# Compression products of a trunk kernel spread over four 32-wide strips of TensorE, with fp32 score masks

## The chip, the cores and the metric

The kernel runs on one core of a Trainium2 chip. The metric is the device time of one execution in microseconds (us). Before the change the median of three runs is 2889.2 us (2888.13 to 2898.22).

## What is computed

A two-layer trunk on 512 tokens of width 2048 (batch 1). Each layer modulates its input, projects it with `w_in`, mixes tokens in three ways side by side (six heads of sparse attention, "NSA", in two key/value groups; six heads of a gated delta rule; four heads of stick-breaking attention), projects with `w_out` and normalizes. The change touches the NSA part. For each of the two groups of a layer:

```python
blk = kv[:, cidx] + pe                   # 31 blocks of 32 tokens, one block every 16 tokens, head dim 128
flat = blk.reshape(31, 32 * 128)
kc or vc = silu(flat @ w1) @ w2          # w1: 4096 x 128, w2: 128 x 128, once for keys, once for values
...
sc = q @ kc.T * scale                    # coarse scores, masked, softmax
ss = q @ ks.T * scale                    # scores on the selected keys, causal mask, softmax
sw = q @ kw.T * scale                    # scores on the window's keys, causal mask, softmax
```

With 512 tokens the selection holds all blocks and the window holds all tokens, so that both of the fine scores are 512 x 512 with a causal mask.

## The kernel before

**The work around the change.** Everything is fp32. The big projections are made of three products with fp32r operands (a high and a low part of each operand). Weights come in one stream: SyncE (SP) loads halves of 128 x 1024 numbers, 512 KB each, into a ring of four slots (`ring`, L391 to L394, in a hardware loop of four loads), and waits before each for its slot's semaphore `raw_free0` to `raw_free3`. For a weight tile GpSimd (POOL) copies a half into `w_hi` and subtracts to get `w_lo` (L1194, L1196), and then frees the slot; TensorE (PE) multiplies eight k-steps of three products by each half (`column_tile`, L450 to L452). A tile is two halves. ScalarE (ACT) copies the finished tile from PSUM (L843, `copy_group`).

**A group's order on PE** (a hardware loop over two groups in each of two layers, so four passes): tile 0 (keys to be compressed), tile 1 (values), `compress(0)`, `compress(1)`, tile 2, the turning of the hidden values, tile 3, the two small `w2` products, tiles 4 to 7, and then three heads, each in 11 steps, between which the remaining six tiles are spread. In the stream the eight halves of `w1` ("D" items: four for keys, four for values) stand behind the halves of tiles 0 and 1, one in each slot for `compress(0)`, then one in each for `compress(1)`, and behind them tiles 2, 3 and so on.

**compress(which)** (L531 to L535) makes 32 products, one for each token of a block: stationary 128 x 31 (`blocks_kv`, made by VectorE, DVE), moving 128 x 128 (`ring`), all added up in `TB[which][0:31]`. It waits for slot q4's load, makes that slot's eight products, and releases the slot:

```python
for q4 in range(4):
    pe.wait_ge(S(f"slot_in{q4}"), ...)
    for i in range(CMP_LEN // 4):
        t = q4 * (CMP_LEN // 4) + i
        last = mm(TB[which][0:N_CMP, 0:HD], blocks_kv..., ring[:, q4, ...], start=(t == 0), ...)
    last.then_inc(S(f"raw_free{q4}"), 1)
```

ACT takes tanh of the sum (L936), DVE makes the silu of it in `hidden` (L1363, L1364), PE turns it (L553) behind tile 2, DVE copies it to `cmpb` (L1367), and PE needs it behind tile 3 (L558).

**The fine scores** (L600, L601): for each head and each of its eight blocks of queries a product of q and keys, 128 x 128 to 128 x 512, and on its last 128 columns a second product that adds the causal mask, `ident_r` times `causal_r`. Both are fp32r copies of constants, which DVE makes once at the start (L1255, L1256). There are 2 layers x 6 heads x 8 = 96 such masks. DVE takes the maximum, ACT the exponential, DVE scales, PE turns (L621) and multiplies by the values (L629).

Of the kernel before, what the change touches and what calls it, by code (L numbers as in the profile page):

```python
# [18 lines left out]
P = 128  # L19
# [103 lines left out]
def constants():  # L123
# [26 lines left out]
    blocks["rot"] = rot  # L150
    inv = np.float32(ROPE_THETA) ** (-np.arange(ROPE_HALF, dtype=np.float32) * np.float32(2.0)
# [11 lines left out]
def build(nc, x, positions, c, b_mod, mod0, small_cols, stream, small, lns, const, out, where, layers=DEPTH):  # L163
    x_norm = nc.dram_tensor("x_norm", (TT, P, DM), F32, kind="Internal").ap()
    ctx = ExitStack()
    with ctx:
# [24 lines left out]
        ident_r = sb("ident_r", [P, P], F32R)  # L191
        causal_r = sb("causal_r", [P, P], F32R)
# [12 lines left out]
        hidden = sb("hidden", [N_CMP, 2, HD])  # L205
# [78 lines left out]
        hid_tanh = A(16, N_CMP)[:, 0:2 * HD].rearrange("p (a n) -> p a n", a=2)  # L284
# [131 lines left out]
        def _(pe):  # L416
# [56 lines left out]
            for l in range(layers):  # L473
# [41 lines left out]
                with pe.Fori(0, KVH) as g:  # L515
# [11 lines left out]
                    def compress(which):  # L527
                        pe.wait_ge(S("blocks_ready"), G * 2 + which + 1)
                        for q4 in range(4):

                            pe.wait_ge(S(f"slot_in{q4}"), (turn_of_group(l, g) + (which + 2)) * 16)  # L531
                            for i in range(CMP_LEN // 4):
                                t = q4 * (CMP_LEN // 4) + i
                                last = mm(TB[which][0:N_CMP, 0:HD], blocks_kv[which][:, t * N_CMP:(t + 1) * N_CMP],
                                          ring[:, q4, i * HD:(i + 1) * HD],  # L535
                                          start=(t == 0), stop=(t == CMP_LEN - 1))
                            last.then_inc(S(f"raw_free{q4}"), 1)
# [12 lines left out]
                    pe.wait_ge(S("hid_ready"), G * 2 + 2)  # L550
                    for which in range(2):

                        last = mm(SB_[which][:, 0:N_CMP], hidden[:, which, :], ident[0:N_CMP, 0:N_CMP],  # L553
                                  start=True, stop=True)
# [21 lines left out]
                    for r in range(GROUP):  # L576
                        H = G * GROUP + r
                        q = qT[r % 2]
                        for s in range(NSA_STEPS):
# [13 lines left out]
                            if 1 <= s <= 8:  # L593
# [7 lines left out]
                                mm(SB_[(u + 1) % 2][:, w - P:w], ident_r[:, :], causal_r[:, :],  # L601
# [238 lines left out]
        def _(act):  # L840
# [34 lines left out]
            for l in range(layers):  # L875
# [37 lines left out]
                with act.Fori(0, KVH) as g:  # L913
# [19 lines left out]
                    for which in range(2):  # L933

                        act.wait_ge(S("raw_free3"), after("raw_free3", turn_of_group(l, g) + (which + 2)))
                        fn(hid_tanh[:, which, :], TB[which][0:N_CMP, 0:HD], ACT.Tanh, scale=0.5)\  # L936
                            .then_inc(S("cmp_tanh"), 1)
                    copy_group(2, kS)
                    copy_group(3, v_raw[0])
                    act.wait_ge(S("cmp_done"), G + 1)  # L940
                    fn(cmpb[:, 0, 0:N_CMP], SB_[0][:, 0:N_CMP], ACT.Copy)
                    fn(vcmp[0:N_CMP, :], SB_[1][0:N_CMP, 0:HD], ACT.Copy)
# [293 lines left out]
        def _(dve):  # L1236
# [18 lines left out]
            cp(ident_r[:, :], ident)  # L1255
# [533 lines left out]
```

## Time and profile before

| | |
|---|---|
| three runs | 2889.2 us median (2888.13 to 2898.22) |
| profiled execution | 2894.21 us, span in the trace 2892.4 us, mean granted TensorE clock 0.959 |
| PE busy | 2557.2 us (88%) |
| PE weight loads | 2016.3 us (70%) |
| DVE busy | 1381.7 us (48%) |
| POOL busy | 1209.2 us (42%) |
| ACT busy | 646.9 us (22%) |
| HBM | 303.92 MB read, 108 GB/s over the span |

The page of the profile gives busy time by engine and, below, instructions in groups by line of the kernel. L843 and L1240 are lines of helpers through which all ACT and nearly all DVE instructions go, so their tiles tell them apart.
### The profile page before, as it was taken

What the parts mean: (1) busy time and instruction counts of PE and PEld (TensorE: products, weight loads), DVE (VectorE), ACT (ScalarE), POOL (GpSimd) and SP (SyncE); (2) the same over time, 40 slices, a digit from 0 to 9 for tenths busy, and PEclk for the clock granted to TensorE, in tenths of its full rate; (3) what the DMA queues carried; (4) which work ended last, traced back from release to release, by engine and by line L of the source; (5) the groups of instructions that cost most, each with busy time, mean ns of one, the idle gap of its engine ahead of it and who ended that gap; (6) DMA issues with size and microseconds to landing.
All of it is one profiled execution on the core that took longest, in us unless ns stands there. A gap on an engine that the chain in (4) does not pass through costs nothing.

```text
span 2892.4 us, 40548 instructions
## 1 busy us (share of the span) xinstructions
PE 2557.2 (88%) x14320; PEld 2016.3 (70%) x14320; DVE 1381.7 (48%) x1915; ACT 646.9 (22%) x1168; POOL 1209.2 (42%) x692
## 2 busy tenths in 40 slices
PE   0499879988999999998987999999899999997994
PEld 0387667666777777776875777777677777775784
DVE  8614751575555553564234143135555554447435
ACT  0201210112222222343003022012222222335000
POOL 7134234323333333544652533443333334443564
PEclk9999989998999999998998999999999999998997
DMA  9533443343111112445323311421111111335531
GB/s 360 220 115 109 135 151 124 124 146 109 59 59 59 60 62 73 157 152 171 95 69 116 124 60 53 131 66 52 59 59 59 59 59 59 124 131 167 184 107 73
DMA packets 82901, 314.81 MB, mean 109 GB/s; under 512 B 9974, under 2 KB 10230, under 8 KB 76950
## 3 DMA queue, kind: packets, MB, share of 16 engines
q1 hardware_dynamic: 76608, 295.51, 31.1%
q10 hardware_dynamic: 6108, 16.83, 1.6%
q8 instruction: 116, 1.90, 0.3%
q14 instruction: 69, 0.57, 0.1%
HBM read 303.92 MB, written 8.39 MB: 108 GB/s over the span
## 4 chain that ended last, share of the span: by engine, by line
PE 68%; DVE 18%; issue 5%; ACT 4%; POOLq 2%; DVEq 1%; ACTq 1%; DMA 0%; SPq 0%
PE bank L450 14%; PE bank L452 13%; PE bank L451 13%; DVE arena L1240 11%; DVE acc L1240 4%; PE bank L831 4%; PE bank L833 4%; PE bank L832 4%; PE bank L430 2%; ACT arena L843 2%; DVE tiny L1240 2%; PE bank L600 1%; ACT L843 1%; PE bank L629 1%; POOLq L1197 1%
## 5 line engine op out<-in xcount | busy, mean ns | idle before, releaser
L1194 POOL CAST w_hi<-ring 128x1024 fp32r<-128x1024 f32 (+1 forms) x328 | 347.4, 1059 | 1594.0 <-PE bank L452 1024.5
L450 PE MATMUL bank<-h_hi,w_hi 128*128 128x512 f32 x2048 | 889.0, 434 | 27.6 <-POOLq L1197 24.1
L452 PE MATMUL bank<-h_hi,w_lo 128*128 128x512 f32 x2048 | 819.5, 400 | 0.9 <-issue 0.9
L451 PE MATMUL bank<-h_lo,w_hi 128*128 128x512 f32 x2048 | 819.3, 400 | 0.0
L1196 POOL TENSOR_TENSOR w_lo<-ring,w_hi 128x1024 fp32r<-128x1024 f32 (+1 forms) x328 | 795.9, 2426 | 48.6 <-issue 2.2
L450 PEld LDWEIGHTS bank<-h_hi,w_hi 128*128 128x128 f32 x2048 | 397.9, 194 | 132.6 <-POOLq L1197 26.8
L452 PEld LDWEIGHTS bank<-h_hi,w_lo 128*128 128x128 f32 x2048 | 395.8, 193 | 90.7
L451 PEld LDWEIGHTS bank<-h_lo,w_hi 128*128 128x128 f32 x2048 | 398.0, 194 | 82.1 <-issue 13.5
L843 ACT ACTIVATE arena<-bank 128x512 f32<-128x512 f32 (+6 forms) x352 | 165.8, 471 | 969.2 <-PE bank L452 395.1
L831 PE MATMUL bank<-w_hi,h_hi 128*128 128x512 f32 x512 | 201.2, 393 | 1.9 <-POOLq L1197 1.9
L1240 DVE SCALAR_TENSOR_TENSOR acc<-ring,cact,acc 128x1024 f32<-128x1024 f32 x128 | 183.3, 1432 | 40.3 <-DMA ring<-in_stream 24.3
L833 PE MATMUL bank<-w_hi,h_lo 128*128 128x512 f32 x512 | 199.3, 389 | 0.0
L832 PE MATMUL bank<-w_lo,h_hi 128*128 128x512 f32 x512 | 199.2, 389 | 0.0
L1240 DVE TENSOR_TENSOR arena<-arena,cst 128x256 f32<-128x256 f32 (+3 forms) x160 | 107.2, 670 | 84.9 <-ACT last_CT L843 49.5
L430 PEld LDWEIGHTS bank<-arena 64*64 64x64 f32 x2880 | 95.2, 136 | 72.6 <-issue 55.9
L843 ACT ACTIVATE arena<-bank,tiny 128x512 f32<-128x512 f32 (+3 forms) x132 | 75.4, 571 | 313.3 <-DVE tiny L1240 286.6
L843 ACT ACTIVATE arena<-arena 128x512 f32<-128x512 f32 (+5 forms) x186 | 95.7, 515 | 208.7 <-DVE arena L1240 178.4
L430 PE MATMUL bank<-arena 64*64 64x64 f32 x2880 | 111.2, 224 | 26.8 <-DVEq L1554 20.0
L843 ACT ACT_TABLE_LOAD x91 | 116.8, 1283 | 68.5 <-issue 61.5
L1240 DVE SCALAR_TENSOR_TENSOR arena<-arena 128x512 f32<-128x512 f32 (+1 forms) x82 | 85.8, 1047 | 80.6 <-ACT arena L843 52.9
L1240 DVE TENSOR_TENSOR arena<-bank,yT 128x512 f32<-128x512 f32 x32 | 22.1, 692 | 212.5 <-PE bank L833 210.7
L831 PEld LDWEIGHTS bank<-w_hi,h_hi 128*128 128x128 f32 x512 | 96.1, 188 | 23.9 <-POOLq L1197 3.2
(192 smaller groups left out, 2756.5 us busy)
## 6 DMA issues: line engine op xcount, KB each, us to landing
ring<-in_stream SPq DMA_DIRECT2D x480, 512.0 KB, 3.6
yT<-in_mod SPq DMA_DIRECT2D x32, 1024.0 KB, 6.2
arena<-in_x SPq DMA_DIRECT2D x1, 4096.0 KB, 14.4
arena<-in_x ACTq DMA_DIRECT2D x4, 1024.0 KB, 10.0
x_norm<-arena ACTq DMA_DIRECT2D x4, 1024.0 KB, 9.3
arena<-x_norm ACTq DMA_DIRECT2D x4, 1024.0 KB, 9.5
out<-arena SPq DMA_DIRECT2D x4, 1024.0 KB, 3.9
raw<-in_lns ACTq DMA_DIRECT2D x8, 256.0 KB, 5.6
```

The costliest lines, as they stand in the source:

```text
L430: last = mm(dst[rows, t, :], lhs[rows, t, :], rhs[rows, t, :], start=True, stop=True)
L450: mm(PJ[b][:, :], hi, h_hi[:, k, :], start=(k == 0), stop=False)
L451: mm(PJ[b][:, :], hi, h_lo[:, k, :], start=False, stop=False)
L452: last = mm(PJ[b][:, :], lo, h_hi[:, k, :], start=False, stop=(k == KT - 1))
L600: mm(SB_[(u + 1) % 2][:, 0:w], q[:, w - P:w], keys[:, 0:w], start=True, stop=False)
L831: mm(outs[t][:, :], h_hi[:, k, at], hi, start=(k == 0), stop=False)
L832: mm(outs[t][:, :], h_hi[:, k, at], lo, start=False, stop=False)
L833: last = mm(outs[t][:, :], h_lo[:, k, at], hi, start=False, stop=(k == KT - 1))
L843: made = act.activation(*args, **kw)
L1194: pool.tensor_copy(w_hi[:, par, 0:w], ring[:, slot, 0:w])
L1196: pool.tensor_tensor(w_lo[:, par, 0:w], ring[:, slot, 0:w], w_hi[:, par, 0:w].bitcast(F32), ALU.subtract)
L1240: made = op(*args, **kw)
```

## The change

The 32 products of `compress` are dealt to four strips. Slot q4's eight products go to output partitions 32 x q4 to 32 x q4 + 30, four strips in turn, so that each strip holds the partial sum of one slot. PE waits for all four slots at once, and releases each with its strip's last product, all four at the end. ACT copies all 128 partitions of the partial sums to `cmp_part`; behind tile 2, in the place where `hidden` was turned, PE multiplies by the constant `sum4` (one in row r, column r mod 32), which adds the four strips and turns. ACT's tanh and one DVE instruction now work on the turned sum; the factor 0.5 moves into the copies behind the `w2` products. The masks are added by a product of the fp32 constants, and the two fp32r copies and their two DVE instructions go away. The constants grow by 31 columns.

```diff
@@ -148,6 +148,7 @@
         rot[ROPE_HALF + i, i] = -1.0
         rot[i, ROPE_HALF + i] = 1.0
     blocks["rot"] = rot
+    blocks["sum4"] = (row % 32 == col[:, :N_CMP])
     inv = np.float32(ROPE_THETA) ** (-np.arange(ROPE_HALF, dtype=np.float32) * np.float32(2.0)
                                      / np.float32(2 * ROPE_HALF))
     misc = np.zeros((P, 2))
@@ -188,8 +189,6 @@
         sm_all = sb("sm_all", [P, SMALL_W])
         cact = sb("cact", [P, 2, KT])
         modT = sb("modT", [P, 2, KT])
-        ident_r = sb("ident_r", [P, P], F32R)
-        causal_r = sb("causal_r", [P, P], F32R)
         h_mod = sb("h_mod", [P, 2, KT])
         ea = sb("ea", [P, GDN_H])
         gates = sb("gates", [P, TT, 18])
@@ -202,7 +201,7 @@
         meanvar = sb("meanvar", [P, TT, 2])
         cmpb = sb("cmpb", [P, 6, 32])
         vcmp = sb("vcmp", [P, HD])
-        hidden = sb("hidden", [N_CMP, 2, HD])
+        cmp_part = sb("cmp_part", [P, 2, HD])
 
         def C(name, parts=P):
             at, n = where[name]
@@ -281,7 +280,8 @@
         masked = [narrow(A(14)), narrow(A(14)[:, NW:])]
         lv_n = narrow(A(17))
         lastT = last_CT[:, :].rearrange("p (t n) -> p t n", t=TT)
-        hid_tanh = A(16, N_CMP)[:, 0:2 * HD].rearrange("p (a n) -> p a n", a=2)
+        hid_tanh = A(16)[:, 0:2 * N_CMP].rearrange("p (a n) -> p a n", a=2)
+        hid_sum = SB_[0][:, 0:64].rearrange("p (a n) -> p a n", a=2)[:, :, 0:N_CMP]
 
 
 
@@ -526,15 +526,17 @@
 
                     def compress(which):
                         pe.wait_ge(S("blocks_ready"), G * 2 + which + 1)
-                        for q4 in range(4):
-
+                        for q4 in range(NS):
                             pe.wait_ge(S(f"slot_in{q4}"), (turn_of_group(l, g) + (which + 2)) * 16)
-                            for i in range(CMP_LEN // 4):
-                                t = q4 * (CMP_LEN // 4) + i
-                                last = mm(TB[which][0:N_CMP, 0:HD], blocks_kv[which][:, t * N_CMP:(t + 1) * N_CMP],
+                        for i in range(CMP_LEN // NS):
+                            for q4 in range(NS):
+                                t = q4 * (CMP_LEN // NS) + i
+                                last = mm(TB[which][q4 * 32:q4 * 32 + N_CMP, 0:HD],
+                                          blocks_kv[which][:, t * N_CMP:(t + 1) * N_CMP],
                                           ring[:, q4, i * HD:(i + 1) * HD],
-                                          start=(t == 0), stop=(t == CMP_LEN - 1))
-                            last.then_inc(S(f"raw_free{q4}"), 1)
+                                          start=(i == 0), stop=(i == CMP_LEN // NS - 1))
+                                if i == CMP_LEN // NS - 1:
+                                    last.then_inc(S(f"raw_free{q4}"), 1)
 
                     def rotate(j, x):
 
@@ -547,11 +549,10 @@
                     compress(0)
                     compress(1)
                     load_tile(2)
-                    pe.wait_ge(S("hid_ready"), G * 2 + 2)
+                    pe.wait_ge(S("cmp_parts"), G * 2 + 2)
                     for which in range(2):
 
-                        last = mm(SB_[which][:, 0:N_CMP], hidden[:, which, :], ident[0:N_CMP, 0:N_CMP],
-                                  start=True, stop=True)
+                        last = mm(hid_sum[:, which, :], cmp_part[:, which, :], C("sum4"), start=True, stop=True)
                     last.then_inc(S("hidT_done"), 1)
                     load_tile(3)
                     pe.wait_ge(S("hidT_ready"), G + 1)
@@ -598,7 +599,7 @@
 
                                 pe.wait_ge(S("exp_done"), after("exp_done", H * 8 + max(u - 1, 0)))
                                 mm(SB_[(u + 1) % 2][:, 0:w], q[:, w - P:w], keys[:, 0:w], start=True, stop=False)
-                                mm(SB_[(u + 1) % 2][:, w - P:w], ident_r[:, :], causal_r[:, :],
+                                mm(SB_[(u + 1) % 2][:, w - P:w], ident, C("causal"),
                                    start=False, stop=True).then_inc(S("scores"), 1)
                             if s == 1:
                                 pe.wait_ge(S("cmp_probs"), H + 1)
@@ -931,15 +932,16 @@
                     copy_group(0, v_raw[0])
                     copy_group(1, v_raw[1])
                     for which in range(2):
-
-                        act.wait_ge(S("raw_free3"), after("raw_free3", turn_of_group(l, g) + (which + 2)))
-                        fn(hid_tanh[:, which, :], TB[which][0:N_CMP, 0:HD], ACT.Tanh, scale=0.5)\
-                            .then_inc(S("cmp_tanh"), 1)
+                        for q4 in range(NS):
+                            act.wait_ge(S(f"raw_free{q4}"), after(f"raw_free{q4}", turn_of_group(l, g) + (which + 2)))
+                        fn(cmp_part[:, which, :], TB[which][:, 0:HD], ACT.Copy).then_inc(S("cmp_parts"), 1)
                     copy_group(2, kS)
+                    act.wait_ge(S("hidT_done"), G + 1)
+                    fn(hid_tanh, hid_sum, ACT.Tanh, scale=0.5).then_inc(S("cmp_tanh"), 1)
                     copy_group(3, v_raw[0])
                     act.wait_ge(S("cmp_done"), G + 1)
-                    fn(cmpb[:, 0, 0:N_CMP], SB_[0][:, 0:N_CMP], ACT.Copy)
-                    fn(vcmp[0:N_CMP, :], SB_[1][0:N_CMP, 0:HD], ACT.Copy)
+                    fn(cmpb[:, 0, 0:N_CMP], SB_[0][:, 0:N_CMP], ACT.Copy, scale=0.5)
+                    fn(vcmp[0:N_CMP, :], SB_[1][0:N_CMP, 0:HD], ACT.Copy, scale=0.5)
                     act.drain().then_inc(S("cmp_copied"), 1)
                     copy_group(4, kW)
                     act.wait_ge(S("vT_done"), G * 2 + 1)
@@ -1252,9 +1254,6 @@
                 fill(sums, 0.0).then_inc(S("acc_zero"), 1)
             dve.wait_ge(S("const_in"), 48)
             dve.wait_ge(S("pool_ready"), 1)
-            cp(ident_r[:, :], ident)
-            cp(causal_r[:, :], C("causal"))
-
             dve.wait_ge(S("c_tanh"), 1)
             stt(cact[:, 1, :], cact[:, 0, :], 1.0, cact[:, 1, :], Ad, M)
             ts(cact[:, 1, :], cact[:, 1, :], 0.5, None, M)
@@ -1357,15 +1356,8 @@
                         windows = bass.AP(src.tensor, src.offset, [src.ap[0], [1, CMP_LEN], [CMP_STRIDE, N_CMP]])
                         tt(blocks_kv[which][:, 0:CMP_LEN * N_CMP].rearrange("p (t n) -> p t n", n=N_CMP), windows,
                            over(peT[:, which, :].unsqueeze(2), (P, CMP_LEN, N_CMP)), Ad).then_inc(S("blocks_ready"), 1)
-                    for which in range(2):
-                        dve.wait_ge(S("cmp_tanh"), G * 2 + which + 1)
-                        hid = hidden[:, which, :]
-                        stt(hid, hid_tanh[:, which, :], 1.0, TB[which][0:N_CMP, 0:HD], Ad, M)
-                        ts(hid, hid, 0.5, None, M).then_inc(S("hid_ready"), 1)
-                    dve.wait_ge(S("hidT_done"), G + 1)
-                    for which in range(2):
-                        cp(cmpb[:, 2 + which, 0:N_CMP], SB_[which][:, 0:N_CMP])
-                    sync().then_inc(S("hidT_ready"), 1)
+                    dve.wait_ge(S("cmp_tanh"), G + 1)
+                    stt(cmpb[:, 2:4, 0:N_CMP], hid_tanh, 1.0, hid_sum, Ad, M).then_inc(S("hidT_ready"), 1)
                     first = CMP_LEN - 1
                     rope(G * 6, cmpb[0:32, 0, 0:N_CMP], N_CMP, slice(first, first + (N_CMP - 1) * CMP_STRIDE + 1, CMP_STRIDE))
                     rope(G * 6 + 1, kS[0:32, :], SEQ, slice(0, SEQ))
```

PE's instructions at the start of a group, behind tile 1 (L534 is the compression product; `slot_in0` to `slot_in3` are the loads). Before:

```order
L531 ISA [waits blocks_ready]
L534 MATMUL bank<-ring,arena 31x128 [waits slot_in0]
L534 MATMUL bank<-ring,arena 31x128 x7
L534 MATMUL bank<-ring,arena 31x128 [waits slot_in1]
L534 MATMUL bank<-ring,arena 31x128 x7
L534 MATMUL bank<-ring,arena 31x128 [waits slot_in2]
L534 MATMUL bank<-ring,arena 31x128 x7
L534 MATMUL bank<-ring,arena 31x128 [waits slot_in3]
L534 MATMUL bank<-ring,arena 31x128 x7
```

and now:

```order
L530 ISA [waits blocks_ready]
L534 MATMUL bank<-ring,arena 31x128 [waits slot_in2,slot_in3,slot_in1,slot_in0]
L534 MATMUL bank<-ring,arena 31x128 x31
L528 REGISTER_ALU
L530 ISA [waits blocks_ready]
L534 MATMUL bank<-ring,arena 31x128 [waits slot_in2,slot_in3,slot_in1,slot_in0]
L534 MATMUL bank<-ring,arena 31x128 x31
```

The number of products is the same; the four waits stand together before the first of them.

ACT's instructions between the copies of tiles 1 and 3 (128x512). Before, from the copy of tile 1 on:

```order
L843 ACTIVATE arena<-bank 128x512 [waits split_used]
L935 ISA
L843 ACTIVATE arena<-bank 31x128 [waits raw_free3]
L935 REGISTER_ALU
L843 ACTIVATE arena<-bank 31x128 [waits raw_free3]
L849 REGISTER_ALU
L843 ACTIVATE arena<-bank 128x512 [waits split_used]
```

and now:

```order
L844 ACTIVATE arena<-bank 128x512 [waits split_used]
L936 ISA
L844 ACTIVATE cmp_part<-bank 128x128 [waits raw_free2,raw_free3,raw_free1,raw_free0]
L936 REGISTER_ALU
L844 ACTIVATE cmp_part<-bank 128x128 [waits raw_free2,raw_free3,raw_free1,raw_free0]
L850 REGISTER_ALU
L844 ACTIVATE arena<-bank 128x512 [waits split_used]
L939 REGISTER_ALU
L844 ACTIVATE arena<-bank 128x62 [waits hidT_done]
L850 REGISTER_ALU
```

The tanh has moved behind the copy of tile 2, where it waits for the turning product.

## Rows read from the trace of the kernel before

**Rows 1.** The page: busy time by engine, and the chain that ended last.

```profile
PE 2557.2 (88%) x14320; PEld 2016.3 (70%) x14320; DVE 1381.7 (48%) x1915; ACT 646.9 (22%) x1168; POOL 1209.2 (42%) x692
...
PE 68%; DVE 18%; issue 5%; ACT 4%; POOLq 2%; DVEq 1%; ACTq 1%; DMA 0%; SPq 0%
```

**Rows 2.** Timeline of PE, first group: start us, us, engine, line, operands, records.

```profile
169.93 0.39 PE L452 MATMUL bank<-h_hi,w_lo 128*128 128x512 f32 x1
170.25 14.16 PE L534 MATMUL bank<-ring,arena 128*31 128x128 f32 x128
187.51 0.50 PE L450 MATMUL bank<-h_hi,w_hi 128*128 128x512 f32 x1 [3.10 <-POOLq L1197]
```

**Rows 3.** Timeline of POOL, first group, behind the compression products.

```profile
183.89 1.04 POOL L1194 CAST w_hi<-ring 128x1024 fp32r<-128x1024 f32 x1 [19.41 <-DMA ring<-in_stream]
185.07 2.34 POOL L1196 TENSOR_TENSOR w_lo<-ring,w_hi 128x1024 fp32r<-128x1024 f32 x1
```

**Rows 4.** Timeline of SP's queue, stretches of 1 us: loads issued in the first group.

```profile
172.37 0.33 SPq L394 DMA_DIRECT2D ring<-in_stream  x1
174.10 0.33 SPq L394 DMA_DIRECT2D ring<-in_stream  x1
...
179.35 0.33 SPq L394 DMA_DIRECT2D ring<-in_stream  x1
```

**Rows 5.** DMA view, loads issued at 172 to 179 us: KB each, median us to landing.

```profile
ring<-in_stream SPq DMA_DIRECT2D x4, 512.0 KB, 4.4
```

**Rows 6.** DMA view, four loads issued at 1150.1, 1151.0, 1151.6 and 1152.2 us.

```profile
ring<-in_stream SPq DMA_DIRECT2D x1, 512.0 KB, 3.4
ring<-in_stream SPq DMA_DIRECT2D x1, 512.0 KB, 5.8
ring<-in_stream SPq DMA_DIRECT2D x1, 512.0 KB, 6.4
ring<-in_stream SPq DMA_DIRECT2D x1, 512.0 KB, 7.2
```

**Rows 7.** Stretches: length, busy us (instructions), granted clock, DMA share, GB/s.

```profile
184.50:187.50 3.00, 0.00 (x0) 0.00 (x0) 2.66 (x2) 0.21 (x1) 2.76 (x2) 1.00 0.82 279
187.50:188.40 0.90, 0.89 (x3) 0.73 (x4) 0.00 (x0) 0.00 (x0) 0.68 (x1) 0.87 0.54 218
188.40:191.40 3.00, 3.00 (x8) 2.32 (x7) 0.00 (x0) 0.00 (x0) 2.73 (x2) 0.50 0.58 180
```

**Rows 8.** Timeline of PE, 726.5 and 729.3 us: 64-wide products in two quarters of the array.

```profile
726.51 0.27 PE L430 MATMUL bank<-arena 64*64 64x64 f32 x2
...
729.35 1.15 PE L430 MATMUL bank<-arena 64*64 64x64 f32 x32 [0.57 <-ACT arena L843]
730.43 0.50 PE L450 MATMUL bank<-h_hi,w_hi 128*128 128x512 f32 x1
```

**Rows 9.** Timeline of PE, a score, its mask and what follows, 291.7 us.

```profile
291.69 0.59 PE L600 MATMUL bank<-arena 128*128 128x256 f32 x2
291.93 0.41 PE L601 MATMUL bank<-causal_r,ident_r 128*128 128x128 f32 x1
...
292.48 1.06 PE L629 MATMUL bank<-arena 128*128 128x128 f32 x8
```

**Rows 10.** Waits of PE in layer 0's groups, 170 to 700 us: us, times, longest.

```profile
PE bank L621 <- DVE arena L1240: 31.8, 23, 3.0
```

**Rows 11.** Waits of PE in layer 1's groups, 1540 to 2100 us.

```profile
PE bank L621 <- DVE arena L1240: 2.6, 6, 0.5
```

**Rows 12.** Timelines of DVE and ACT, first group: the blocks of values; the copies of tiles 2 and 3.

```profile
170.99 1.86 DVE L1240 TENSOR_TENSOR arena<-arena,sm_all 128x992 f32<-128x992 f32 x1 [8.72 <-ACT arena L843]
...
200.33 0.60 ACT L843 ACTIVATE arena<-bank 128x512 f32<-128x512 f32 x1 [15.62 <-PE bank L452]
212.00 0.60 ACT L843 ACTIVATE arena<-bank 128x512 f32<-128x512 f32 x1 [11.07 <-PE bank L452]
```

**Rows 13.** The group of compression weight loads: duration min/median/max ns.

```profile
L534 PEld LDWEIGHTS bank<-ring,arena x512: 104/109/110, 170.2 to 1833.2; 128*31 128x31 f32 x171
```

**Rows 14.** DMA view of the opening stretch, 16 to 60 us.

```profile
DMA packets 2209, 16.11 MB, mean 366 GB/s; under 512 B 242, under 2 KB 242, under 8 KB 242
```

## The prediction

> **What bounds the kernel now.** I read the page first. PE is busy for 88% of the span, and the chain that ended last runs through PE for 68% of it [rows 1], so PE's time counts unless PE waits for something else at that place. The change touches two places, so I then read PE's timeline at both. In the first group 32 + 32 compression products start at 170.25 and stream until about 184.3; PE then stands idle for 3.10 us until POOL has split the first half of tile 2, and goes on at 187.51 [rows 2]. From the first compression product to the first product of tile 2 that is 17.26 us (the other groups read the same within 0.3 us; I take 17.3). What that end waited for is in POOL's timeline: its cast at 183.89 ended an idle time of 19.41 us and was released by a ring load, and cast plus subtraction took 3.6 us [rows 3]. That load was issued at 179.35, when the first quarter of `compress(1)` had released slot 0 [rows 4], and landed 4.5 us later. So this stretch does not end on PE's products: it ends on a chain of slot release, load, split. PE's 14.16 us of products are mostly the cover under which the eight loads run.
>
> **Compression, step by step (per group, four groups).**
>
> Now: 64 records per `compress`, two `compress` calls, 128 records in 14.16 us, so 0.109 us of spacing each (128 columns at two cycles), 7.0 us per call [rows 2]. How well four strips overlap, the trace before does not show; the nearest rows are the 64-wide products in two quarters of the array. There two records start within 0.27 us including their drain, and 32 records pass in 1.08 us [rows 8], 0.034 us each, or 0.058 us for a pair where one alone needs 64 x 2 / 2.4 GHz = 0.053 us. Two quarters overlap almost wholly. Bounds for a call are therefore 7.0 us (no overlap) and 64 / 4 x 0.109 = 1.75 us (four at once); I take 1.8 us, by the quarters.
>
> Released slots: before, a slot was released every 1.75 us and its load issued at once (172.37, 174.10, ... [rows 4]), landing 4.4 us later in the median [rows 5], all under running products. Now all four are released with the end of the call, and `compress(1)` waits for all four. Its `w1` halves cannot be loaded earlier, since the four slots hold those of `compress(0)`. So the loads lose their cover:
>
> - `compress(0)`: 1.8 us.
> - last product out, semaphore, issue: 0.4 us (the first 16 records stream until 172.0, the load is issued at 172.37).
> - four loads in a burst. The trace has such a burst: issued within 2.0 us, they land 3.4, 5.8, 6.4 and 7.2 us after their own issue [rows 6], the last 9.2 us after the first issue. A fifth load shared the end of that burst; from below, 2.1 MB at the opening stretch's 366 GB/s [rows 14] is 5.7 us, plus the 2.0 us by which a lone load's 3.4 exceeds its own 1.4, is 7.7 us. I take the middle, 8.4 us.
> - `compress(1)`. PE has idled for almost 9 us by then. Behind the idle time of 3.0 us before tile 2 the granted clock fell to 0.50, that is 1.2 GHz, for 188.4 to 191.4 [rows 7]. So I take 3.5 us at the slow clock; the bound from below is 1.8.
> - release and issue 0.4 us; the first half of tile 2, again first of a burst of four: 3.4 us [rows 6] to 4.6 (the steady stream here), I take 4.0; POOL's split 3.6 us [rows 3].
>
> Sum: 1.8 + 0.4 + 8.4 + 3.5 + 0.4 + 4.0 + 3.6 = 22.1 us against 17.3, so +4.8 us. The longer idle time before tile 2 (8 us, not 3.1) also makes the slow stretch start with its first product; before, it cost 7 products at 0.43 instead of 0.23 us, 1.4 us. I add 1.0 us, an estimate between nothing and twice that. That is +5.8 us per group, +23 us for four. PE's busy time falls by about 10 us per group and none of it reaches the end.
>
> The Trainium skill ("TensorE: Matmul & The Clock Gate", Part 3) gives 2.38-fold for three 32-column strips, not three-fold. Scaled to four strips, an estimate, it would make a call 2.2 us and the sum 4 to 5 us larger; no row here shows strips.
>
> **The masks.** 96 times an fp32r product becomes an fp32 one. Before, the fp32r record ends 0.05 us after the fp32 score before it (291.93 + 0.41 against 291.69 + 0.59) [rows 9]; over all 96 the least and usual difference is 0.06 us, and 128 columns at 2.4 GHz are 0.053. An fp32 product of the same shape is two records, and eight such records take 1.06 us less the 0.275 us of one, over seven steps: 0.11 us each [rows 9]. So 0.22 instead of 0.06 us, +0.16 us, 15.4 us for all 96 if each counts. In layer 1's groups PE hardly waits in this part [rows 11]: 48 x 0.16 = 7.7 us. In layer 0's groups it waited 23 times, 31.8 us, for DVE's probabilities [rows 10], since DVE also sums the next layer's modulation; there a later PE partly finds the wait shorter, and I count half, 3.8 us. Together 12 us (bounds 5 and 15.4).
>
> **Costed at nothing.** The turning product has the same four records with the same 128-column weight loads; it needs `cmp_part`, ready a few tenths after `compress(1)`, while PE still has tile 2 ahead. ACT's tanh and DVE's one instruction come behind the copy at 200.33 and are needed behind tile 3 at about 212 [rows 12]: under 2 us of work under 11 us of products. Were that cover gone, those 2 us would be paid per group. DVE's blocks of values, 1.86 us from 170.99 [rows 12], end later than the short `compress(0)`, but well within its burst; with landed loads they would be the next wait. On SP's queue nothing else stands behind the held-back loads that is needed sooner. The 31 constant columns are 16 KB, under 0.1 us at the start; the two DVE casts lie under the opening loads.
>
> **Sum.** 23 + 12 = +35 us on the profiled execution's 2894.2 us (span 2892.4) gives 2929. That execution is 5 us above the median of 2889.2, so I forecast 2925 us for the median.
>
> **Rivals.**
>
> *Two at a time.* A product is two records in one strip, and if PE starts records strictly in order, a strip's second record holds back the next strip, which leaves twofold overlap. With two quarters this would look as it does now except for the first pair, which starts together [rows 8]; that speaks against it. Calls 3.5 and some 6 us: 3.5 + 0.4 + 8.4 + 6 + 0.4 + 4.0 + 3.6 = 26.3, +9, with the clock +10 per group, +40, with the masks 2941.
>
> *The strips don't overlap.* The quarters of [rows 8] differ in rows as well as columns, the strips share all 128 rows. If strips on the same rows run one after another, the calls stay at 7.0 and, partly at the slow clock, 9.5 us, the burst stands in full between them: 33.3 us, +17 per group with the clock, +68, with the masks 2969. Against it: weight loads of 104 to 109 ns [rows 13] already hide under products on the same rows at a spacing of 109 ns, so loading need not stop the array. The Trainium skill has the rule for it: "TensorE: Matmul & The Clock Gate", Part 3, says that a weight load overlaps with running products only when its row group differs. By that rule the forecast would be this rival's; [rows 13] does not bear it out for neighbouring records.
>
> *Not slower: the burst is short.* If the four loads are issued 0.6 us apart and land as in the steady stream, the last is there after 1.8 + 4.6 = 6.4 us; if the clock also stays at 2.4 GHz and the next load lands in 3.4, the stretch is 1.8 + 0.4 + 6.4 + 1.8 + 0.4 + 3.4 + 3.6 = 17.8 us, +0.5 per group, and masks hidden under waits leave some 2 more: 2893. It decides the case when the burst takes under about 6.5 us. For it: the stream ran at over 290 GB/s here. Against it: the measured burst [rows 6]. I find no mechanism that reaches a gain, since even four-fold strips leave two exposed loads.
>
> **Chances and range.** Forecast's mechanism 0.66, its own range 2901 (burst 7.7, fast clock, masks 5) to 2937 (burst 9.2, load 4.6, masks 15.4, slow stretch doubled); two at a time 0.10; no overlap 0.12; not slower 0.12. The range 2900 to 2950 holds the first two and leaves out the third and most of the last. A measurement tells 0.5%, 14.4 us, from no change. Below 2903.6 lie the last rival and a sliver of the first case: same 0.14; faster 0.03 for what I don't see; slower 0.83.
>
> **What would show it.** PE's idle time inside L534 of 8 to 9 us per group, released by ring loads, and some 7 to 8 us before tile 2 where 3.1 were; loads issued in fours; L534's records at about 0.03 us of spacing (0.055: twofold; 0.109: none); from the first compression product to tile 2 22 us; L602 with 192 records at 0.11. Wrong would be: that stretch at or under 17.3 us, four loads landing within 6.5 us, or masks that leave the heads' stretches unchanged.

## The result and the profile after

The changed kernel takes 2915.2 us in the median of four runs (2912.9 to 2915.9), the kernel before 2891.8 beside it; the ratio is 1.0065, with a 95% interval of 1.0047 to 1.0083, some 19 us slower. The profiled execution has a span of 2913.3 us. TensorE (PE) is busy for 34 us less than before and the time is longer. In the page, the busy times and the largest groups:

```profile
PE 2523.3 (87%) x14416; PEld 1987.7 (68%) x14416; DVE 1370.0 (47%) x1893; ACT 649.5 (22%) x1172; POOL 1209.8 (42%) x692
...
L450 PE MATMUL bank<-h_hi,w_hi 128*128 128x512 f32 x2048 | 885.6, 432 | 49.4 <-POOLq L1199 45.9
```

**The compression stretch.** PE's timeline of the first group, against [rows 2]:

```profile
168.69 1.96 PE L534 MATMUL bank<-ring,arena 128*31 128x128 f32 x64
179.15 3.64 PE L534 MATMUL bank<-ring,arena 128*31 128x128 f32 x64 [8.51 <-DMA ring<-in_stream]
190.26 0.80 PE L450 MATMUL bank<-h_hi,w_hi 128*128 128x512 f32 x1 [7.46 <-POOLq L1199]
```

The first call's 64 records take 1.96 us where before a call took 7.0. Then PE waits 8.51 us for the ring, makes the second call in 3.64 us, and waits 7.46 us for POOL. From the first compression product to tile 2 it is 21.57 us, before 17.26. The four groups read 21.6, 22.9, 21.5 and 21.5 against 17.3, 17.5, 17.0 and 17.1: 18.7 us more in sum.

SyncE's queue issues the four loads in a row, against one every 1.75 us in [rows 4] (timeline, short stretches):

```profile
170.81 0.33 SPq L394 DMA_DIRECT2D ring<-in_stream  x1
171.33 0.35 SPq L394 DMA_DIRECT2D ring<-in_stream  x1
171.88 0.33 SPq L394 DMA_DIRECT2D ring<-in_stream  x1
172.40 0.33 SPq L394 DMA_DIRECT2D ring<-in_stream  x1
```

They land 3.8 to 6.6 us after their issue, the last at about 179.0, 8.2 us after the first issue. POOL's timeline behind the second call shows the same 3.6 us of split as [rows 3]:

```profile
186.63 1.04 POOL L1196 CAST w_hi<-ring 128x1024 fp32r<-128x1024 f32 x1 [23.73 <-DMA ring<-in_stream]
187.82 2.34 POOL L1198 TENSOR_TENSOR w_lo<-ring,w_hi 128x1024 fp32r<-128x1024 f32 x1
```

The granted clock by stretch (length, busy times with counts, clock, DMA share, GB/s):

```profile
170.70:179.10 8.40, 0.00 (x0) 0.00 (x0) 0.59 (x1) 0.28 (x1) 0.00 (x0) 0.81 0.70 250
179.10:182.70 3.60, 3.55 (x64) 3.22 (x64) 0.00 (x0) 0.00 (x0) 0.00 (x0) 0.50 0.00 0
182.80:190.20 7.40, 0.00 (x0) 0.00 (x0) 0.00 (x0) 0.28 (x1) 3.38 (x2) 0.73 0.78 282
190.20:196.40 6.20, 6.14 (x14) 4.79 (x15) 0.00 (x0) 0.00 (x0) 3.41 (x2) 0.50 0.44 133
```

The columns behind the length are PE, PE's weight loads, DVE, ACT and POOL. The second call runs wholly at 1.2 GHz (granted clock 0.50), and so do the first 6 us of tile 2; in [rows 7] it was 3 us. The DMA share is 0.70 while PE waits for the ring and 0.00 while it makes the second call: there loads and products take turns.

**The masks.** Groups of PE by shape, and a score with its mask in layer 1:

```profile
L602 PE MATMUL bank<-cst 128*128 128x128 f32 x192 | 37.4, 277 | 0.0
```

```profile
1756.84 0.59 PE L601 MATMUL bank<-arena 128*128 128x256 f32 x2
1757.27 0.38 PE L602 MATMUL bank<-cst 128*128 128x128 f32 x2
1757.49 0.27 PE L622 MATMUL bank<-cst,arena 128*128 128x128 f32 x1
```

The mask now ends 0.22 us after the score in front of it (1757.27 + 0.38 against 1756.84 + 0.59), where it was 0.06 in [rows 9]. The ends of a layer 1 group's three heads, in PE's timeline, before:

```profile
1678.31 0.96 PE L590 MATMUL bank<-cmpb,arena 128*128 128x31 f32 x7 [1.91 <-DVE arena L1240]
...
1793.75 0.94 PE L629 MATMUL bank<-arena 128*128 128x128 f32 x7
```

and after:

```profile
1693.67 0.85 PE L591 MATMUL bank<-cmpb,arena 128*128 128x31 f32 x6 [1.90 <-DVE arena L1242]
...
1811.74 1.05 PE L630 MATMUL bank<-arena 128*128 128x128 f32 x8
```

116.4 us have become 119.1; the other group of layer 1 gains the same 2.7 us. In layer 0 the same stretches changed by +0.8 and -0.1 us. PE's waits for DVE in front of the turning product of layer 0 did not shrink for it (170 to 710 us; 31.8 us in [rows 10]):

```profile
PE bank L622 <- DVE arena L1242: 33.6, 25, 2.6
```

All of PE's idle time in the two stretches (length less busy time) is 45.7 us, before 46.8.

So the trace puts 18.7 us into the four compression stretches and 5.4 us into layer 1's heads. The other stretches sum to -3 us, in lumps of up to 3 us where no instruction changed.

### The profile page after: what moved, and what is told of

It reads as the page before. It is cut to its first block, busy times and chain, and to the rows that moved or that the text cites. A ratio compares the mean times of both kernels' runs of the same rounds, so it can differ in the third digit from the quotient of the medians.

```text
span 2913.3 us, 40724 instructions
## 1 busy us (share of the span) xinstructions
PE 2523.3 (87%) x14416; PEld 1987.7 (68%) x14416; DVE 1370.0 (47%) x1893; ACT 649.5 (22%) x1172; POOL 1209.8 (42%) x692
## 4 chain that ended last, share of the span: by engine, by line
PE 67%; DVE 19%; issue 6%; ACT 4%; POOLq 2%; DVEq 1%; ACTq 1%; DMA 0%; SPq 0%
PE bank L450 14%; PE bank L452 13%; PE bank L451 13%; DVE arena L1242 11%; DVE acc L1242 5%; PE bank L832 4%; PE bank L833 4%; PE bank L834 4%; PE bank L430 2%; ACT arena L844 2%; DVE tiny L1242 2%; ACT L844 1%; PE bank L630 1%; PE bank L601 1%; POOLq L1199 1%
## 5 line engine op out<-in xcount | busy, mean ns | idle before, releaser
L844 ACT ACTIVATE arena<-bank 128x512 f32<-128x512 f32 (+4 forms) x348 | 165.2, 475 | 928.3 <-PE bank L452 408.9
L844 ACT ACTIVATE arena<-bank,tiny 128x512 f32<-128x512 f32 (+3 forms) x132 | 75.7, 574 | 320.0 <-DVE tiny L1242 294.6
L1242 DVE TENSOR_TENSOR arena<-bank,yT 128x512 f32<-128x512 f32 x32 | 22.1, 692 | 212.9 <-PE bank L834 210.8
```

The lines of the kernel that those rows point to most:

```text
L844: made = act.activation(*args, **kw)
L1242: made = op(*args, **kw)
```

## The experiments

All times are medians; "before" is the kernel before on the same chip. Stretches are read from PE's timeline as above.

**One half of the change each.** The kernel before with

```diff
-mm(SB_[(u + 1) % 2][:, w - P:w], ident_r[:, :], causal_r[:, :], ...)
+mm(SB_[(u + 1) % 2][:, w - P:w], ident, C("causal"), ...)
```

> The kernel before with its 96 score masks as fp32 products, nothing else changed. Theory (each mask costs 0.16 us more on TensorE, 222 instead of 60 ns; layer 0's are hidden under the waits for VectorE, layer 1's mostly paid): 5 to 6 us slower than before, all of it in layer 1's two head stretches (+2.7 us each), and layer 0's head stretches within 1 us. Rival (the masks cost nothing on the way to the end and the +2.7 us came from the shifted clock): within 1 us of before in layer 1's head stretches. Rival (my forecast's half share in layer 0): +12 us in all.

Measured: 2894.8 against 2893.8, ratio 1.0003 (0.9990 to 1.0015). Layer 1's head stretches are +2.6 us each, as expected, layer 0's -0.2 and -1.1.

The changed kernel with the line the other way round:

> The changed kernel with the masks as fp32r products again, so strips, joint waits, joint release and turned sum alone. Theory (the stretch from the first compression product to tile 2 grows from 17.2 to about 21.9 us because eight loads lose their cover): 17 to 20 us slower than before, 5 to 6 us faster than the changed kernel. Rival (clock and other things carry part of it): under 14 us slower than before.

Measured: 2908.0, ratio 1.0054 (1.0034 to 1.0074), 15.6 us slower by the ratio. The four stretches are 17.3 us longer in its trace, and every head stretch is within 0.7 us of before. It is 7 us under the changed kernel by medians, 3 by ratios. The time falls between the theory (17 to 20) and the rival (under 14), while the trace gives nearly the theory's stretches. The strips carry most of the loss.

**The order of the products.** The changed kernel with the two loops exchanged and each slot's wait and release inside:

```diff
-for i in range(8):
-    for q4 in range(4):                      # strip q4
+for q4 in range(4):                          # wait for slot q4
+    for i in range(8):                       # strip q4, then release slot q4
```

> The changed kernel (fp32 masks) with the products in the order of before: slot by slot, each slot's eight products in its one strip, wait and release per slot; the turned sum stays. Theory (the order takes away both the overlap of the strips and the burst; the new path behind it is free): L534 at 0.11 us spacing again, the stretch back at 17.3 us, the time equal to that of the kernel before with fp32 masks, about 5 us over before. Rival (the turned sum, the later tanh or the four-strip outputs cost something): over 10 us over before.

Measured: 2886.8 against 2893.8, ratio 0.9969 (0.9958 to 0.9981). The rival falls: the path behind the products costs nothing. But the theory missed too: it had the kernel 5 us over before, and it is 7 to 9 us under. The stretch is not 17.3 us: it is 16.2 us in the first group and 1.0 us shorter than before on average. That is 4 us; where the rest of the gain comes from is not shown (the mean granted clock of its twelve runs is 0.966, of the kernel before beside it 0.961). Its loads, in SyncE's timeline, are 1.34 us apart instead of 1.75:

```profile
173.54 0.33 SPq L394 DMA_DIRECT2D ring<-in_stream  x1
174.87 0.33 SPq L394 DMA_DIRECT2D ring<-in_stream  x1
176.21 0.33 SPq L394 DMA_DIRECT2D ring<-in_stream  x1
```

Around 172.8 us PE's records show why: where the products of the next strip come up, some start between the last ones of the strip in front (0.03 us behind one of them instead of 0.11): the first record of the strip that waits for slot 1 starts at 172.76, the last one of the strip in front, which releases slot 0, at 173.09. So even eight products in one strip overlap a little with their neighbours.

The same with fp32r masks:

> As the slot-by-slot kernel with one strip per slot, but fp32r masks. That kernel was 7 us faster than before, of which 4 us are its shorter compression stretches. Theory (the masks' 5 us in layer 1's heads are real and what is left, some 8 us, is in slow-clock stretches elsewhere that differ from execution to execution and kernel to kernel): 5 us faster than that kernel, 2881 to 2883. Rival (fp32 masks keep TensorE busier and so spare slow-clock time, which pays for them): equal to that kernel or slower, 2886 to 2890, that is 4 to 7 us faster than before.

Measured: 2884.3 against 2894.3, ratio 0.9972 (0.9960 to 0.9985); by the ratio that is the time of the kernel above, by the median 2.5 us less. Neither theory is clean here. Its trace has a second gain: in three of the four groups the clock stays up behind PE's wait for tile 2. The first:

```profile
185.08 0.50 PE L452 MATMUL bank<-h_hi,w_hi 128*128 128x512 f32 x1 [2.90 <-POOLq L1199]
185.42 0.40 PE L453 MATMUL bank<-h_lo,w_hi 128*128 128x512 f32 x1
```

```profile
180.00:200.00 20.00, 17.10 (x91) 14.29 (x90) 0.22 (x1) 1.10 (x3) 13.66 (x8) 1.00 0.50 169
```

Before, 3.10 us of idle time were followed by the slow 3 us of [rows 7]; in the three groups with the fast clock the way from tile 2 to the heads is 1.8 to 1.9 us shorter. But the length of the wait does not decide it here: the kernel above waited 2.96 us in its third group and the clock fell, this one waited 2.96 us in its third and it did not. So this gain of some 6 us belongs to the profiled execution. It came in one of four groups of the kernel above and of the first kernel with fp32 masks alone, and in none of the eight groups in the two profiles of the kernel before; how often it comes is open.

**Slots in turn, all four strips in each.**

```diff
+for q4 in range(4):                          # wait for slot q4
+    for i in range(8):                       # strip i % 4, then release slot q4
```

> Fp32r masks, and each slot's eight products dealt over the four strips, slots in turn, wait and release per slot. Theory (what counts is when slots are released, and the eight loads in a row are the bound): each slot takes about 0.45 us, loads are issued about 0.5 us apart from 0.9 us on, so compress(1) is done as its loads land, the load for tile 2 is issued some 5 us after the start and lands at about 10.5, tile 2 starts at about 14.5 us instead of 17.3: 10 us faster than before (4 x 2.8), down to nothing if the slow clock takes it back. Rival (release time does not matter, the burst of four costs its 8 to 9 us in any case and the next burst follows it): as the strips alone, 17 us slower than before.

Measured: 2880.9, ratio 0.9955 (0.9939 to 0.9972), 13 us faster than before. The stretches are 14.2, 14.0, 14.8 and 14.7 us, against 14.5 expected. The same strips and the same overlap lose 16 us when all slots are waited for and released together and gain 13 when they are taken in turn. The rival is excluded. The wait and the release changed together here, so what each is worth is not separated.

**Taking the burst away.** The changed kernel with four of the eight `w1` halves left out of the stream (the values' products read the keys' halves), and slots released behind `compress(1)` alone:

> The changed kernel without the four loads of the values' w1: the values' products use the same four halves as the keys' (so the values' compression is made with the wrong half of the weights), the slots are released only behind them. It makes the same products and leaves out 2 MB of loads per group and the wait for them. Theory (the stretch of 21.9 us holds 8.5 us of wait for the burst and 1.7 us of slow clock behind it): compress(1) starts at about 2.8 us, when VectorE's blocks of values are ready, and the stretch is 2.8 + 1.8 + 0.4 + 3.7 + 3.6 = 12.3 us; 38 us faster than the changed kernel, 2876 to 2880 us. Rival (the wait would only move in front of tile 2, POOL or the next loads being the bound): under 20 us faster than the changed kernel.

Measured: 2873.2, ratio 0.9919 (0.9894 to 0.9943), 42 us under the changed kernel, where 38 were expected. The first group:

```profile
170.46 1.95 PE L534 MATMUL bank<-ring,arena 128*31 128x128 f32 x64
173.11 1.96 PE L534 MATMUL bank<-ring,arena 128*31 128x128 f32 x64 [0.69 <-DVE arena L1242]
182.53 0.80 PE L450 MATMUL bank<-h_hi,w_hi 128*128 128x512 f32 x1 [7.47 <-POOLq L1199]
```

12.1 us, 12.3 expected: the second call starts when DVE's blocks are there, runs at the fast clock, and the 7.5 us of load and split stay. The burst and the slow clock behind it are worth 9.8 us per group on average, 39 us of the 42.

**Pricing the masks.** The kernel before with fp32 masks, each made three times:

```diff
+for _ in range(2):
+    mm(SB_[(u + 1) % 2][:, w - P:w], ident, C("causal"), start=False, stop=False)
 mm(SB_[(u + 1) % 2][:, w - P:w], ident, C("causal"), start=False, stop=True)
```

> The kernel before with fp32 masks, each mask product made three times (the added constant is 0 or -1e30, so the scores keep their meaning). Two more products per mask, 0.222 us each: 96 x 0.444 = 42.6 us of TensorE's time. Theory (layer 1 pays, layer 0 hides it under VectorE's chain as long as that has room): layer 1's head stretches +10 us each beyond the single fp32 mask (some 12 to 13 against before), layer 0's at most +5 each; 22 to 30 us slower than before in all. Rival (all of it on the path everywhere, the single mask was only masked by clock noise): 45 to 50 us slower. Rival (masks always hide): under 5 us.

Measured: 2923.4, ratio 1.0105 (1.0086 to 1.0125), 29 us over before. Layer 1's head stretches are +12.5 and +12.4 us, where 24 masks at 0.16 + 0.44 us would be 14.5: some 85% is paid. Layer 0's are +2.2 and +1.4 us for the same work. The two head stretches of layer 0 before:

```profile
265.14:410.81 145.67, 121.51 (x577) 94.37 (x577) 103.48 (x169) 31.02 (x83) 42.90 (x23) 0.93 0.50 159
535.63:682.04 146.41, 123.75 (x577) 96.11 (x577) 103.61 (x169) 31.03 (x83) 42.20 (x23) 0.91 0.49 158
```

and here:

```profile
265.02:412.94 147.92, 129.47 (x697) 103.97 (x697) 103.33 (x169) 31.06 (x83) 43.93 (x23) 0.98 0.47 157
538.13:685.97 147.84, 129.43 (x697) 104.00 (x697) 103.23 (x169) 31.07 (x83) 43.46 (x23) 0.98 0.47 157
```

The 48 masks add 48 x 0.6 = 29 us of products. PE's idle time (length less busy time) falls from 46.8 to 36.9 us, and the stretches grow by 3.7 us: that takes up 14 us, by which PE's busy time grows. The other 15 us appear nowhere, because the granted clock is 0.98 instead of 0.93 and 0.91 and the same products take less time. So in layer 0 the larger part of the masks' price comes back as clock, the smaller part as shorter waits.

**Chance or give-back?** To see how much of a profile is chance I ran the kernel before as a control, and the masks alone again.

> The kernel before, unchanged, as a control. Theory (which stretches run at the slow clock differs from execution to execution): the ratio is 1 within its interval, and its profiled execution differs from the first one by up to a few us in single stretches that no kernel of this study touches, as the gated delta rule's, with a sum of slow-clock time that is not the same 188 us. Rival (the slow stretches are a fixed property of the program): every stretch within 0.3 us of the first profile.

Measured: ratio 0.9999 (0.9984 to 1.0013). Its profiled execution spans 2899.8 us, not 2892.4. Stretches with the same instructions differ by -2.9 us (layer 0's gated delta rule), +3.8 us (behind it), +2.7 us (the start of layer 1) and +1.4 us (layer 0's second head stretch), while all four compression stretches agree within 0.2 us and layer 1's head stretches within 0.04. So those lumps are chance, and the two kinds of stretch on which the account rests agree.

> The kernel before with fp32 masks, a second time. The first gave a ratio of 1.0003 with an upper end of 1.0015 (4 us), where its own trace showed +2.6 us in each of layer 1's head stretches. Theory (5 us are paid in those stretches, the rest is chance): this time 1 to 7 us slower than before, head stretches +2.6 us again. Rival (fp32 masks give back in slow-clock time what they cost): equal to before within 2 us, and less slow-clock time than the control in the head stretches of layer 0.

Measured: ratio 1.0004 (0.9991 to 1.0016). Layer 1's head stretches are +2.6 and +1.0 us, layer 0's -0.2 and -1.5. The two of layer 1:

```profile
1682.22:1801.22 119.00, 115.17 (x601) 91.76 (x601) 56.38 (x137) 31.08 (x83) 38.67 (x23) 0.99 0.17 54
1920.23:2037.66 117.43, 113.61 (x601) 90.63 (x601) 56.08 (x137) 31.09 (x83) 38.66 (x23) 1.00 0.17 54
```

The +1.0 is no smaller price. In the first of them the clock falls for some 3 us behind PE's wait of 1.9 us in front of the heads, in the second it does not, which is worth 1.6 us. The same stretch has two lengths in all the traces: 116.4 or 114.8 us with fp32r masks, some 119.0 or 117.4 with single fp32 masks. The masks cost 2.6 us in either case. Two intervals now end at 4.5 us, so the 5 us of the trace are not wholly in the time. Layer 0's second head stretch is 1.1 and 1.5 us shorter than in the first profile and 2.5 and 2.9 shorter than in the control. There PE is granted more clock with fp32 masks. The stretches 265 to 415 and 540 to 690 us (layer 0's heads) in the control:

```profile
265.00:415.00 150.00, 125.83 (x598) 98.22 (x598) 103.97 (x171) 31.05 (x83) 44.35 (x24) 0.92 0.48 155
540.00:690.00 150.00, 123.61 (x596) 96.90 (x594) 101.63 (x165) 31.06 (x83) 44.31 (x24) 0.92 0.49 158
```

and with fp32 masks, second run:

```profile
265.00:415.00 150.00, 126.49 (x623) 99.92 (x623) 104.64 (x171) 31.05 (x83) 45.15 (x24) 0.94 0.47 155
540.00:690.00 150.00, 127.09 (x625) 100.81 (x624) 102.69 (x167) 30.76 (x82) 44.93 (x24) 0.93 0.48 157
```

The single runs say the same: the mean granted clock is 0.964 and 0.963 in the 23 runs with fp32 masks, and 0.961 in those of the kernel before beside them (0.960 in the control). Together with the tripled masks this shows that most of layer 0's price comes back as clock; over the whole kernel the single masks cost some 1 us by both ratios, in intervals that reach from -3 to +5.

**A version that beats both.** If the loads' cover is the matter, the `w1` halves belong under the tiles' products. In the stream, two stand in front of each of tiles 2 to 5, so that they take slots 0 and 1 while tiles keep 2 and 3:

```diff
-items = mixed((0, 1), 0) + [("D", i) for i in range(8)] + mixed(range(2, 8), 0)
+items = mixed((0, 1), 0)
+for i in range(4):
+    items += [("D", 2 * i), ("D", 2 * i + 1)] + mixed((2 + i,), 0)
+items += mixed((6, 7), 0)
```

PE makes 16 products in front of each of these tiles, each slot's over the four strips; turned sum, `w2` products and the rotations move two tiles later, and the waits of ACT and DVE with them.

> Four strips, fp32r masks, and the eight w1 halves in pairs between the tiles of the weight stream (two in front of each of the tiles 2 to 5), so that the compression products are made in four pieces of 0.9 us, and every load and POOL's splits run under the tiles' products. Theory (the stretch was bound by release, load and split, not by products): the 17.3 us of products and waiting per group become 3.6 to 4.5 us, the slow-clock stretch behind it goes too: 50 to 58 us faster than before, 2836 to 2844 us. Rival (loads of the pairs are late, since SyncE issues them only when the pair before is released and in order): waits of 3 to 7 us in front of tiles 3 to 5, under 20 us faster than before.

Measured: 2829.2 against 2894.3, ratio 0.9771 (0.9756 to 0.9787): 65 us faster than before, where 50 to 58 were expected. PE's timeline around the second piece, and the stretch of all four pieces:

```profile
177.69 0.39 PE L460 MATMUL bank<-h_hi,w_lo 128*128 128x512 f32 x1
178.01 1.08 PE L544 MATMUL bank<-ring,arena 128*31 128x128 f32 x32
179.02 0.50 PE L458 MATMUL bank<-h_hi,w_hi 128*128 128x512 f32 x1
```

```profile
165.90:205.00 39.10, 39.10 (x280) 30.79 (x280) 3.77 (x3) 3.32 (x7) 24.33 (x14) 1.00 0.46 162
```

PE is busy in all of 39.1 us, at the full clock; the way from the first compression product to the heads is 79.8 us instead of 94.9 in the first group, and 15 us shorter in each; that is 60 us. Another 3 us of the profile are layer 1's head stretches, both of which have the shorter of their two lengths here.

> The same order of the stream and of the pieces, with all products in one strip as before the change. Theory (with the loads covered, the products' own time is what is left, 3.5 us per piece): 14 us per group, slower than the kernel with strips by 4 x 10.4 = 42 us, faster than before by 10 to 20 us. Rival (the gain is all in the order, strips give nothing): within 5 us of the kernel with strips.

Measured: 2872.9, ratio 0.9923 (0.9908 to 0.9938), 21 us faster than before. A piece takes 3.68 us instead of 1.08, and 16 pieces make 42 of the 44 us between the two kernels. So the strips are worth 44 us where the loads are covered; in the changed kernel, where they are not, the same strips lose 16.

> The kernel with the w1 halves between the tiles, with fp32 masks: the whole change in the new order of the stream. Theory (the masks cost 2.6 us in each of layer 1's head stretches whatever stands in front): 3 to 6 us slower than the same kernel with fp32r masks, 2832 to 2836 us. Rival (they cost nothing on average): within 1.5 us of it.

Measured: 2835.2, ratio 0.9796 (0.9773 to 0.9818), 6 us over the same kernel with fp32r masks by medians. Layer 1's head stretches are +2.7 us against before, +4.3 against that kernel, of which 1.6 each is the clock that fell here and not there; layer 0's are 1.0 and 1.9 us shorter than in that kernel. It is the third pair of traces in which they are not longer with fp32 masks; between the changed kernel and the strips alone, the first one is 1.5 us longer.

## Why the prediction was right, and where it was not

The direction, the place and the mechanism of the compression stretches were right; 2915 lies in the range of 2900 to 2950, and the forecast of +35 us was too large by about a third or more (+19 by the ratio, +23 by medians). The stretches brought what was forecast for them; most of the excess is in two smaller terms, the masks and the clock behind tile 2's wait.

- **Four at a time.** 1.8 us forecast for a call, 1.96 us including the drain measured, with four records starting together every 0.11 us. Twofold overlap and no overlap fall, and so does the prediction's estimate of 2.2 us for a call. The rule cited from the Trainium skill ("TensorE: Matmul & The Clock Gate", Part 3), that weight loads overlap with running products only for another row group, does not hold for these strips: they share all rows, and the 64 weight loads of the first call lie within its 1.96 us, beside the 64 products.
- **The burst.** 8.4 us forecast from its four nearest loads, 8.2 measured in the first group. PE's wait is 8.5 to 8.6 us in three groups and 9.8 in the second.
- **The second call** at the slow clock: 3.5 forecast, 3.64 with drain. Load 4.0 forecast, 3.7 measured; split 3.6 and 3.6.
- **The sum of the stretch**: 22.1 us forecast, 21.9 on average measured. This term, +4.8 us per group, was right.
- **The clock behind it**, +1.0 us per group on top: mis-sized. From tile 2 to the heads the four groups changed by +1.0, +0.3, -0.3 and +0.3 us, 1.4 in sum where I had 4. With the fast clock the same way takes 75.7 us (the slot-by-slot kernel with fp32r masks), so before it had already lost 1.8 to 1.9 us in each group, not 1.4, and the changed kernel loses 1.6 to 2.9.
- **The masks**, 12 us: the unit price (+0.16 us) was right, the share was not. In layer 1 I counted all of 7.7 us and 5.4 appear; in layer 0 I counted half, 3.8 us, where +0.8 and -0.1 us appear, although unchanged heads' stretches stood among the prediction's own signs of being wrong. The step that failed is "there a later PE partly finds the wait shorter, and I count half". The waits got 1 us shorter (45.7 us of idle time against 46.8), where 7.7 us of products were added; PE got a higher clock in those stretches (0.95 and 0.93, before 0.93 and 0.91), which the sum does not have. Over the whole kernel the masks' price by the ratios of the runs is 1 us twice where they are alone, 3 us on the strips, 7 us in the new order of the stream and -1 us slot by slot, against 12 forecast.
- **Costed at nothing**: the path behind the products indeed costs nothing, as the slot-by-slot kernels show.
- **The working**: the low end of the forecast's own range, 2901, does not come out of the three terms that it names, which give 2904; it also needs the next load at 3.4 us. 2889.2 and 35 are 2924, not 2925.
- "I find no mechanism that reaches a gain" holds for this change, but two orders of the same products reach one.

## What to carry to other kernels

Before making products faster, ask what ends the stretch: if it is a chain of slot release, load and preparation, products are cover, and faster ones that release their slots together turn cover into waits. Keep releases staggered through any reordering, and put the data of a short burst of products into the stream between long ones. Price an added instruction on each path apart: the same 24 masks cost 2.6 us where PE is the bound, and between -3 and +1.5 us where PE waits for another engine. There they took little of the waits; PE was granted more clock instead, and this must be read from the clock of the stretch and not from the waits.

## What was not expected of the hardware

- PE starts products of another strip before earlier ones of the strip in front have started (172.76 against 173.09 us in the slot-by-slot kernel); eight products in one strip, followed by eight in the next, took 1.34 us per slot instead of 1.75.
- Waits of 2.4 to 3.3 us in front of tile 2 were followed by 3 us at 1.2 GHz in some groups and not in others (2.96 us at the same place with either outcome), at 1.8 us each. Behind the waits of 7 to 8 us the clock was low every time.
- In front of the heads of layer 1 even a wait of 1.9 us was followed by some 3 us at 1.2 GHz in most traces and by none in others, at 1.6 us each.
- Where PE has many short waits (layer 0's heads), 24 to 120 more short records per stretch went with a higher granted clock: 0.91 to 0.93 with fp32r masks, 0.93 to 0.95 with fp32 masks, 0.98 with three of them.
- Two executions of the same program differ by up to 4 us in stretches of a few hundred us. In layer 0's gated delta rule the 2.9 us are all PE's busy time, with the clock at 0.99 in one and 1.00 in the other; the others hold waits as well. Of two profiles only stretches that repeat can be compared to a tenth.
